# Down projections and most of an up projection as seven quarter products instead of eight, in a two-block float32 kernel on one core

## The reference

```python
# block one, d_ff = 4096
hf = rmsnorm(x, g_norm[l, 4])
yf = jnp.square(jax.nn.relu(hf @ w_up[l])) @ w_down[l]
x = x + rmsnorm(yf, g_norm[l, 5])
# block two, 16 meta tokens in front (272 tokens), twice, D_FF_2 = 2816
def conv_glu_ffn(x, w_up, conv_w, conv_b, w_down):
    u = x @ w_up
    ...
    gate, val = jnp.split(u, 2, axis=-1)
    return (jax.nn.silu(gate) * val) @ w_down
h = h + conv_glu_ffn(rms_norm(h, norm_ffn_g[layer]), ...)
```

## Time and profile before

| | us |
|---|---|
| median of the runs | 1638.88 (3 runs, 1638.53 to 1639.74) |
| the profiled execution | 1636.88 |
| its span | 1634.8 |
| TensorE busy in it | 1536.2 |
| VectorE busy | 527.2 |
| ScalarE busy | 343.8 |

### The profile page before, as it was taken

The page is one execution under the profiler, slowest core; times in us unless marked ns, Lnnn a source line. Parts: engine busy times, 40 slices in busy tenths (PEclk is TensorE's granted clock), DMA queues, the critical chain, the costliest instruction groups (busy, mean ns, idle before and its releaser), DMA issues.

```text
span 1634.8 us, 25810 instructions
## 1 busy us (share of the span) xinstructions
PE 1536.2 (94%) x10548; PEld 1290.2 (79%) x10548; DVE 527.2 (32%) x977; ACT 343.8 (21%) x613; POOL 30.3 (2%) x47
## 2 busy tenths in 40 slices
PE   8999999989999879998888999999998879999997
PEld 6888788988888758577774888888886768888886
DVE  2140233331100273547535244431112542444301
ACT  1231103231100112200111223310102652323101
POOL 0130000000000000000000000000001100000000
PEclk9999999999999999899997999999999669999999
DMA  8444243354444304130000444444443003444441
GB/s 333 143 129 154 77 143 115 132 185 154 150 146 154 115 26 129 52 104 4 4 3 0 142 142 142 144 151 155 149 147 116 0 0 116 143 143 148 144 155 52
DMA packets 54435, 189.75 MB, mean 116 GB/s; under 512 B 6961, under 2 KB 9137, under 8 KB 53970
## 3 DMA queue, kind: packets, MB, share of 16 engines
q1 hardware_dynamic: 50480, 180.67, 33.3%
q10 hardware_dynamic: 3874, 7.85, 1.5%
HBM read 187.45 MB, written 1.05 MB: 115 GB/s over the span
## 4 chain that ended last, share of the span: by engine, by line
PE 89%; DVE 6%; issue 3%; ACT 1%; DMA 0%; POOL 0%; DVEq 0%; ACTq 0%; SPq 0%; PEldq 0%; POOLq 0%
PE ps L1365 88%; DVE arena L1165 1%; DVE arena L1193 0%; DVE arena L1302 0%; DMA ring<-in_stream 0%; DVE rs L1829 0%; DVE arena L1306 0%; DVE arena L1192 0%; DVE arena L1007 0%; DVE arena L999 0%; DVE res L1838 0%; DVE arena L997 0%; DVE arena L1846 0%; DVE arena L1315 0%; ACT L1648 0%
## 5 line engine op out<-in xcount | busy, mean ns | idle before, releaser
L1365 PE MATMUL ps<-arena,ring 128*128 128x272 f32 (+2 forms) x5504 | 1212.1, 383 | 19.7 <-DMA ring<-in_stream 8.2
L1365 PEld LDWEIGHTS ps<-arena,ring 128*128 128x128 f32 x5504 | 1028.3, 192 | 201.9 <-issue 16.0
L1365 PE MATMUL ps<-arena 64*64 64x64 f32 (+7 forms) x3828 | 177.8, 246 | 46.0 <-DVE arena L1315 12.2
L1365 PEld LDWEIGHTS ps<-arena 64*64 64x64 f32 (+3 forms) x3828 | 142.1, 141 | 80.8 <-issue 42.0
L1365 PE MATMUL ps<-arena,consts 128*128 128x16 f32 (+7 forms) x438 | 116.3, 425 | 19.9 <-DVE arena L1306 6.0
L1365 PEld LDWEIGHTS ps<-arena,consts 128*128 128x128 f32 (+3 forms) x438 | 84.8, 234 | 47.3 <-DVE arena L1306 6.1
L910 ACT ACTIVATE arena<-arena,cols 128x272 f32<-128x272 f32 x88 | 53.7, 613 | 184.5 <-DVE arena L1130 184.3
L1137 DVE SCALAR_TENSOR_TENSOR arena<-arena,cols 128x271 f32<-128x271 f32 (+1 forms) x176 | 84.1, 498 | 15.1 <-ACT arena L910 3.2
L1130 DVE TENSOR_TENSOR arena<-ps,rs 128x272 f32<-128x272 f32 x88 | 38.9, 442 | 149.5 <-PE ps L1365 147.7
L1079 DVE TENSOR_TENSOR res<-res,ps 128x272 f32<-128x272 f32 x32 | 14.0, 439 | 194.6 <-PE ps L1365 194.6
L891 ACT ACTIVATE arena<-res 128x272 f32<-128x272 f32 x32 | 13.8, 430 | 212.2 <-DVE res L1079 212.2
(11 more groups left out here) (219 smaller groups left out, 692.1 us busy)
## 6 DMA issues: line engine op xcount, KB each, us to landing
ring<-in_stream SPq DMA_DIRECT2D x342, 512.0 KB, 3.2
consts<-in_consts ACTq DMA_DIRECT2D x1, 1516.0 KB, 8.5
arena<-in_x_t ACTq DMA_DIRECT2D x1, 1024.0 KB, 5.8
arena<-in_mem_t ACTq DMA_DIRECT2D x1, 1024.0 KB, 4.8
res<-in_x_t ACTq DMA_DIRECT2D x1, 1024.0 KB, 14.2
out_t<-arena SPq DMA_DIRECT2D x4, 256.0 KB, 3.0
arena<-in_g ACTq DMA_DIRECT2D x1, 640.0 KB, 5.6
arena<-in_w ACTq DMA_DIRECT2D x2, 256.0 KB, 4.8
```

The source lines that it names most:

```text
L1365: return nc.tensor.matmul(out, lhs, rhs, start=start, stop=stop)
```

## The change

**What is computed.** A product of a 2x2 arrangement of weight tiles with a 2x2 arrangement of inputs takes eight tile products, or seven with sums made before and after (Winograd's form of Strassen's scheme). Here the 2x2 of the weights are two neighbouring outputs by two neighbouring input tiles; the 2x2 of the inputs are those two input tiles by two halves of the tokens (128 and 128, or 136 and 136, `T2`). With weights a and inputs b, `seven_products` does

```diff
@@ seven_products and its sums, new
+        def seven_products(pe, mm, name, second=None):
+            y = SEVEN[name]
+            b11, b12, b21, b22 = x_quarters(name)
+            t1, t2, t3, t4 = x_summed_quarters(name)
+            x_of = {1: b11, 2: b21, 3: b22, 4: t4, 5: t1, 6: t2, 7: t3}
+            lead, end = [{y.place[p][0]: p for p in order} for order in (ORDER[::-1], ORDER)]
+            for i in range(y.i0, y.n):
+                if y.off + 2 * (i - 1) > 0:
+                    pe.wait_ge(ev[name], y.off + 2 * (i - 1))
+                if second and i == y.i0 + 1:
+                    second()
+                for g, n in enumerate(y.groups):
+                    b, done = y.block(i, g), 4 * y.group(i, g)
+                    s1, s2, s3, s4 = [WSUM[name][y.group(i, g) % 2][:, x] for x in range(4)]
+                    a11, a12, a21, a22 = w_quarters(b)
+                    w_of = {1: a11, 2: a12, 3: s4, 4: a22, 5: s1, 6: s2, 7: s3}
+                    arrived(pe, b)
+                    arrived(pe, b + 1)
+                    if i == y.i0:
+                        pe.wait_ge(x_summed, y.sums0 + {"down": g + 1, "ffa_down": 2 * g + 2, "ffb_down": 2 * g + 2
+                                                        }.get(name, SHARED.get(name, 1)))
+                    for p in ORDER:
+                        if p in (6, 7, 3):
+                            pe.wait_ge(w_summed, done + {6: 2, 7: 3, 3: 4}[p])
+                        bank = y.place[p][0]
+                        for l in range(n):
+                            last = mm(product_at(y, i, p), w_of[p][:, l, :], x_of[p][:, 4 * g + l, :],
+                                      g == 0 and l == 0 and p == lead[bank],
+                                      g == len(y.groups) - 1 and l == n - 1 and p == end[bank])
+                        if g == len(y.groups) - 1 and p in (6, 4, 2):
+                            last.then_inc(products, 1)
+                    last.then_inc(used, 2)
...
+        def weight_sums(dve, tt, name, i, g):
...
+            arrived(dve, b)
+            arrived(dve, b + 1)
+            if b - 4 >= y.block(y.i0) or not y.own:
+                dve.wait_ge(used, b - 2)
+            tt(s1, a21, a22, ALU.add).then_inc(w_summed, 1)
+            dve.wait_ge(w_summed, done + 1)
+            tt(s2, s1, a11, ALU.subtract).then_inc(w_summed, 1)
+            tt(s3, a11, a21, ALU.subtract).then_inc(w_summed, 1)
+            dve.wait_ge(w_summed, done + 2)
+            tt(s4, a12, s2, ALU.subtract).then_inc(w_summed, 1)
+
+        def x_sums(link, tt, name, at=slice(None)):
+            b11, b12, b21, b22 = [x[:, at, :] for x in x_quarters(name)]
+            t1, t2, t3, t4 = [x[:, at, :] for x in x_summed_quarters(name)]
+            link(tt(t1, b12, b11, ALU.subtract))
+            link(tt(t2, b22, t1, ALU.subtract))
+            tt(t3, b22, b12, ALU.subtract)
+            tt(t4, b21, t2, ALU.subtract).then_inc(x_summed, 1)
+
+        def seven_vector(dve, tt, name, quads, then=None):
+
+            y = SEVEN[name]
+            work = [(name, i, g) for i in range(y.i0, y.n) for g in range(len(y.groups))]
+            if then:
+                work.append((then, SEVEN[then].i0, 0))
+            for at, (_, i, g) in enumerate(work):
+                if at + 1 < len(work):
+                    weight_sums(dve, tt, *work[at + 1])
+                if g == 0 and at and at < len(work) - bool(then):
+                    quads(i - 1)
+            quads(y.n - 1)
@@ quads_to_res, new: recombination in block two (the end of a pair)
+                dve.wait_ge(products, 3 * y.pair(i) + 3)
+                tt(e[1], e[1], pr(5), ALU.add).then_inc(ev[name], 1)
+                link(tt(o[1], o[1], pr(5), ALU.add))
+                tt(o[0], o[0], pr(2), ALU.add)
+                if i:
+                    link(add_squares(2 * i))
+                dve.wait_ge(used, y.block(i + 1))
+                tt(o[1], o[1], pr(3), ALU.add).then_inc(ev[name], 1)
+                if i == 3:
+                    add_squares(7).then_inc(sq_added, 1)
@@ ffn_vector: sums of the inputs of block two's down projections
             with dve.Fori(0, 5) as it:
-                link.enter(it, 8)
+                link.enter(it, 10)
                 for m in range(4):
                     pair(m, it)
+                dve.wait_ge(ffm, it * 4 + (layer * (2 + F2) + 2 + 4))
+                x_sums(link, tt, name + "_down", bass.ds(it * 2, 2))
                 link.leave(5)
+            weight_sums(dve, tt, name + "_down", 0, 0)
             for m in (20, 21):
                 pair(m)
+            dve.wait_ge(ffm, layer * (2 + F2) + 2 + F2)
+            x_sums(link, tt, name + "_down", slice(10, 11))
@@ TensorE, block one
-            tiles("up", FIRST["up"] + UH, FF - UH, h, S, j0=UH, after=total_hf)
-            pe.wait_ge(ev["up"], GB + FF)
-            pe.wait_ge(up_sq, GB + FF)
...
+            pe.wait_ge(ev["up"], GB + 3)
+
+            def fourth():
+                pe.wait_ge(ev["up"], GB + UH)
+                total_hf()
+            seven_products(pe, mm, "upq", fourth)
+            pe.wait_ge(ev["upq"], FF - UH - 2)
+            seven_products(pe, mm, "down", lambda: pe.wait_ge(ev["upq"], FF - UH))
@@ VectorE, block one
             residual_ym(1)
+            tail_act.wait(dve, "hf1", 8)
+            x_sums(link, tt, "upq")
+            weight_sums(dve, tt, "upq", UH // 2, 0)
             tail_act.wait(dve, "hf_sq", 2)
...
+            def quads_squared(i):
...
+                dve.wait_ge(used, y.block(i + 1))
+                dve.wait_ge(p1_kept, y.pair(i) + 1)
+                link(tt(u2, p1, product_at(y, i, 6), ALU.add))
+                tt(quarters[:, 2, :], p1, product_at(y, i, 2), ALU.add)
+                link(tt(uv, two(7), over(u2, 2), ALU.add))
+                tt(quarters[:, 0:4:3, :], uv, two(4), ALU.add)
+                tt(quarters[:, 1, :], uv[:, 0, :], product_at(y, i, 5), ALU.add).then_inc(ev["upq"], 2)
+                dve.wait_ge(ev["upq"], 2 * (i + 1) - UH)
+                dst = act_up[:, 2 * i:2 * i + 2, :].rearrange("p a (b t) -> p (a b) t", b=2)
+                stt(out=dst, in0=quarters, scalar=0.0, in1=quarters, op0=ALU.max, op1=ALU.mult).then_inc(up_sq, 1)
+                if i == UH // 2 + 1:
+                    tail_pe.wait(dve, "hf_summed")
+                    link(ts(rs2, ps[:, 7, 0:S], EPS, None, ALU.add))
+                    link(v.reciprocal(rs2, rs2))
+                if i % 4 == 3:
+                    dve.wait_ge(up_sq, GB + UH + i + 1 - UH // 2)
+                    x_sums(link, tt, "down", slice(i - 3, i + 1))
+            seven_vector(dve, tt, "upq", quads_squared, then="down")
+
+            def quads_to_y(i):
...
+                dve.wait_ge(products, 3 * y.pair(i) + 3)
+                link(tt(e[1], u3, pr(5), ALU.add))
+                tt(y1[:, 2 * i, :], y1[:, 2 * i, :], rs2, ALU.mult).then_inc(ev[name], 1)
+                link(tt(u4, u2, pr(5), ALU.add))
+                tt(o[0], p1, pr(2), ALU.add)
+                dve.wait_ge(used, y.block(i + 1))
+                link(tt(o[1], u4, pr(3), ALU.add))
+                tt(y1[:, 2 * i + 1, :], y1[:, 2 * i + 1, :], rs2, ALU.mult).then_inc(ev[name], 1)
```

More of the change, by code:

```diff
@@ L157, in wait, with block, pair, group @@
         eng.wait_ge(self.sem, self.at[name] + n)
+@dataclass
+class Seven:
+    first: int
+    t: int
+    groups: list
+    banks: tuple
+    place: dict
+    i0: int
+    n: int
+    off: int
+    own: bool
+    pair0: int = 0
+    group0: int = 0
+    sums0: int = 0
+    def block(self, i, g=0):
+        return self.first + 2 * (len(self.groups) * i + g)
+    def pair(self, i):
+        return self.pair0 + i - self.i0
+    def group(self, i, g):
+        return self.group0 + len(self.groups) * (i - self.i0) + g
 class Space:
@@ L2038, in _ @@
[L2038 to L2048 removed]
+            for s in range(UH):
+                dve.wait_ge(ev["up"], GB + s + 1)
+                tt(act_up[:, s, :], tmp[:, s % 4, :], tmp[:, s % 4, :], ALU.mult).then_inc(up_sq, 1)
```

312 lines of the change are left out of this document (198 added, 114 removed).

## The result

| | before | after |
|---|---|---|
| median of the runs, us | 1639.31 (4 runs, 1638.53 to 1642.63) | 1601.33 (4 runs, 1599.97 to 1602.88) |
| the profiled execution | 1636.88 | 1600.63 |
| its span | 1634.8 | 1598.9 |

The ratio of after to before is 0.9765 (95% interval 0.9748 to 0.9782): 38 us less. The forecast was 1601.4.

A forecast was written before the change was run, and what follows sets the result against it. TensorE, busy 94% of the span, was taken as the bound. Savings of 18.9 + 18.7 + 1.5 less 0.7, 0.4 and 0.5 gave 37.5 us: 1636.9 to 1599.4, plus 2.0 for the median, 1601.4; range 1597 to 1610 us.

The forecast's parts named there:

- Block one's squares: Block one's up and down projections: 116 squares, each 163.3 ns shorter with seven narrow matmuls; 18.9 us saved.
- Block two's squares: Block two's two down projections: 88 squares at 136 columns, each 212.0 ns shorter; 18.7 us saved.
- The rival at 236.6 ns: Block two's down projections: a fixed cost makes 136-column matmuls slower, so that saving is 15.6 us, total 1604.5; chance 17%.
- The joint: Between block one's up and down projections: TensorE no longer waits for the last square of the activations; 1.5 us saved.
- Tails: Recombining adds on VectorE after the last matmuls: 0.7 us lost behind block one's down projection, 0.4 at the kernel's end.
- Weight sums: Four VectorE sums of 128x512 for each of 53 groups, 2.56 us a group; nobody waits in the down projections: 0.
- The up projection: Block one's up projection: VectorE is tight, 11.95 of 12.5 us in the worst stretch; 0.5 us booked for stalls.
- The start: Start of block one's up projection: input and first weight sums ready with 1 us of cover; otherwise 0 to 2 us lost.
- SP, ScalarE, banks: SP's load queue, ScalarE's copies replacing relus, and the banks for the stage after block two's first down projection: 0 each.
- VectorE as the bound: Block one's up projection: TensorE waits for VectorE, 2.4 us giving 1603, or 9.8 giving 1611; chance 12%.
- The full eighth: Block one's 116 squares: half the columns take half the time, saving 6.1 us more, total 1595.3; chance 5%.
- Weight loads set the pace: Narrow matmuls: seven loads not hidden under half the columns; decides from 26 ns more per matmul, up to 1826 us; chance 3.5%.

The follow-up runs named there:

- experiment 7: The changed kernel plus an eighth product per square on 64 of the 128 or 136 columns, full weight tile; median 1641.97 us.
- 9: The changed kernel plus an eighth product with half a weight tile (64 output columns) on 64 moving columns, issued sixth of eight; 1641.1 us, one execution.
- experiment 5: The change in block one alone, block two's down projections as in the kernel before; median 1617.83 us, 0.987 of before.
- experiment 4: The changed kernel with three more adds of 128x512 in each group of weight sums of the three down projections; median 1600.16 us.
- experiment 2: The changed kernel with one more add of 128x512 in each group of weight sums of block one's up projection; median 1600.99 us.
- 10: The changed kernel plus an eighth product with half a weight tile (64 output columns) on all 128 or 136 moving columns; 1663.0 us, one execution.
- experiment 8: The changed kernel with the stick-breaking attention's value and query projections by seven products too; median 1592.34 us, 0.9715 of before.

## Why the prediction was right, point by point

The forecast was 1601.4, the median 1601.3. The mechanism was right. That the two agree within 0.1 us is luck: executions of one kernel scatter by 3 us and more, and two misses cancel. The sum for the profiled execution was 1.2 us too low (1599.4 for 1600.6), and the median lay 0.7 us above the profiled execution where 2.0 were added. By its terms:

1. *Block one's squares.* 223.4 ns a matmul where 223.3 was taken; 812 of them without a stall. With terms 3, 4 and 6 this stretch was to save 18.9 + 1.5 - 0.7 - 0.5 = 19.2 us and saved 20.2. (The 21 us that the prediction names among its signs does not follow from these terms.)
2. *Block two's squares.* 231.6 ns at 136 columns, as taken. The rival at 236.6 ns is out. What lifts 128 columns to 223.3 ns is a floor, since 64 columns cost the same (experiment 7), and it goes with the size of the weight tile, since with half a tile the matmul takes 117 ns (9). 136 columns lie past it and on the line of 256 and 272. The last down projection brought 9.3 us (8.9 expected), the first 8.4 (9.35 expected); the missing 0.9 is clock (last section). Against the same stage of experiment 5, whose granted clock at the start was like that of after (0.70 and 0.72), it brought 9.5.
   The Trainium skill's fixed cost of about 2.5 ns behind every warm matmul (TensorE: Matmul & The Clock Gate, Wait — 56ns, not 53.3ns?) does not fall with the rival; what falls is that the prediction counted it four times, once a pass. A float32 matmul leaves two records, so the estimate with the page's figure counted twice is, with four passes at 2.4 GHz, 4 x 136 / 2.4 + 2 x 2.5 = 231.7 ns, 431.7 at 256 columns and 458.3 at 272, where 231.6, 431.6 and 458.3 were measured. At 128 columns it gives 218.3, which is what half a tile takes (218); the full tile takes 5 ns more.
3. *The joint* is closed: the chain has one piece over it. TensorE waited for none of the activation sums.
4. *Tails.* The tail of block one, after:

```profile
538.46 0.29 DVE L2288 TENSOR_TENSOR arena<-arena,ps 128x128 f32<-128x128 f32 x1 [1.11 <-PE ps L1589]
...
539.96 0.42 DVE L2294 TENSOR_TENSOR arena<-arena 128x256 f32<-128x256 f32 x1
```

```profile
540.95 3.72 PE L1589 MATMUL ps<-arena,consts 128*128 128x256 f32 x16 [1.63 <-ACT arena L1938]
```

   The products that the prediction named release the adds in the order it gave, 0.32 us apart where each needs the last; TensorE waited 1.63 us where it had waited 1.25. So 0.4 us was lost, not 0.7. At the end of the kernel:

```profile
1588.96 1.18 PE L1589 MATMUL ps<-arena,consts 128*128 128x272 f32 x4 [1.34 <-DVE arena L1265]
```

   1.34 us in place of 0.95: the 0.4 that was worked out.
5. *Weight sums.* Four in 2.5 us (389.37, then the next operation at 391.91), 2.56 taken. Nobody waits. In the down projections three more adds a group cost 1.6 us in all (experiment 4).
6. *The up projection.* 11.7 us of 12.5 in the worst stretch, 11.95 taken. The 0.5 us booked for stalls were not spent. The room of 0.8 us was real all the same: with 1.2 us of adds more in this stretch TensorE waits (experiment 2).
7. *The start.* The second pair's block landed just in time for VectorE, which waited 0.9 us for it. Its sums were complete at 361.5; TensorE wanted them behind the first four matmuls of the group at 364.06, so at 365.0. So there were 3.5 us to spare, not 1: VectorE came 1 us earlier than worked out and TensorE 1.5 later; the total of the input lies between the groups.

```profile
358.88 0.69 DVE L693 TENSOR_TENSOR arena<-ring 128x512 f32<-128x512 f32 x1 [0.90 <-DMA ring<-in_stream]
...
360.82 0.69 DVE L698 TENSOR_TENSOR arena<-ring,arena 128x512 f32<-128x512 f32 x1
...
364.06 1.05 PE L1589 MATMUL ps<-arena,ring 128*128 128x128 f32 x8
```

8. *SP, ScalarE, banks*: no wait for them showed, as booked.

The rivals. For VectorE as the bound it takes about 0.6 us more work in each group of the up projection (experiment 2). The full eighth fell with the pace of 223.4 ns. *Weight loads set the pace* did not come as it was priced: none of its 26 ns a matmul was lost. Its mechanism is there, though, and the prediction had it only as what "looks like a floor near 223 ns": experiments 7 and 9 tie the floor to the weight tile, and it costs 5 ns at 128 columns, which the 223.3 ns contained. The steady stretch of after fits this (columns as in the earlier trace rows, where before stands):

```profile
460.00:530.00 70.00, 70.00 (x630) 70.00 (x629) 36.76 (x73) 3.14 (x9) 0.00 (x0) 1.00 0.50 172
```

Weight loading was busy for 70.42 of 80 us before, and for all of 70 now. The Trainium skill's figure of about 81 ns for a pair of load and matmul at 128 columns (TensorE: Matmul & The Clock Gate, Back-to-back issue gap) does not hold as the prediction read it, once a pass: 223.4 / 4 = 55.9 ns in 812 matmuls. But the trace has two such pairs to a float32 matmul, 111.7 ns apart, with two passes each, so for a pair of one pass no run here tests the figure.

The sum, 1599.4 for 1600.6, also fits better than its parts: block one brought 1.0 us more than booked and the last down projection 0.4, while the first brought 0.9 less and 2.0 us came in from the stretches in front of and behind block one's, where the work is the same.

## What to carry to other kernels

Here a scheme that drops an eighth of the products took 9.5% off a stream of matmuls at 128 columns and 11.6% at 136. It needs narrow matmuls that stay above the floor that goes with their weight tile (223 ns for 128x128 in float32 at the full clock). Below it more splitting gives nothing, and without the dropped product eight narrow products were slower than four wide ones. Pay for it with an engine that is idle beside the stream, and count its worst stretch between two dues, not its mean share: VectorE, busy for 78% of a pair, had only 0.8 us of room where other sums fall due. Where a difference of 3 us is sought in a kernel whose executions scatter by 3 to 11, read the stretch in the trace: the medians did not show the three waits of experiment 2.

## What the runs showed of the hardware that was not expected

**The change of the load's size costs.** Between 128x128 and 128x64 loads, in and out again, TensorE lost 0.34 us, with 64 and with 128 moving columns alike (experiments 9 and 10). What it waits for there is not shown, and the two runs have one execution each; the ten groups of each are alike, with starts 7.06 and 7.47 us apart.

**TensorE's clock behind a wait differs from execution to execution.** Windows of 10 us from the start of the gated output's projection, PE busy, granted clock, DMA and GB/s; before, after, and block one alone (where this stage is that of before):

```profile
892.87:902.87 10.00, 10.00 (x36) 0.81 0.16 52
```

```profile
874.67:884.67 10.00, 10.00 (x32) 0.72 0.19 54
```

```profile
874.74:884.74 10.00, 10.00 (x31) 0.70 0.17 52
```

TensorE works without a pause in all three, at the half level (1.2 GHz) first, at the full one (2.4 GHz) behind it. In the 2 us before, TensorE stood idle and was granted 0.50 in each. The half level then lasts 4 us in the first, 6 in the others; before is the exception, all other runs have 0.70 to 0.73 here. 10 x (0.81 - 0.72) = 0.9 us of work at the full level is what this down projection lacked in after, and 10 x (0.81 - 0.70) = 1.1 us, by which the same stage was longer in experiment 5 (365.47 against 364.41) though nothing in it had changed. Behind the stick-breaking attention, after and then experiment 8:

```profile
1321.53:1331.53 10.00, 10.00 (x31) 0.70 0.15 52
```

```profile
1312.30:1322.30 10.00, 10.00 (x36) 0.83 0.16 52
```

1.3 us again, in a stage that is the same in both. Here what stood before differs: in the 6 us ahead of this start TensorE was busy for 3.11 us in every run, but at 1.00 in experiments 5, 8, 9 and 10, which then were granted 0.83, and at 0.50 in the others, which were granted 0.70 to 0.74. Over the whole execution the mean granted clock goes roughly with the time: block one alone had spans of 1613.3, 1615.7, 1616.4 and 1621.3 us at 0.961, 0.958, 0.958 and 0.953, but after had its shortest, 1598.2, at 0.957 and 1598.9 at 0.959. What decides between the levels there was not tried.
